# Causal attention of the second block: mask added to the forget sums by GpSimd, the minimum in two parts, reciprocals spread through memory

## The chip, the cores and the metric

The kernel runs on one core of one Trainium2 chip, and its time is the device time of one execution in microseconds (us). Three runs of the kernel before took 2592.71, 2601.61 and 2602.12 us; the median is 2601.61 us. The engines are named as in the profile: PE (TensorE, with PEld for its weight loads), DVE (VectorE), ACT (ScalarE), POOL (GpSimd) and SP (SyncE, which here only issues transfers).

## The reference

Two transformer blocks follow each other on 1024 tokens of width 1024, in float32: a first block with attention and a mixture of experts, and a second block with two attention layers. The change lies in the first layer of the second block, causal attention of 16 heads of 64 columns with forget gates:

```python
log_f = jax.nn.log_sigmoid((f_logit + b_forget[i]).astype(jnp.float32))
c = jnp.cumsum(log_f, axis=1)
...
logits = jnp.einsum('bqhd,bkhd->bhqk', qi, k) * scale
logits = logits + ci[..., :, None] - c_k[..., None, :]
causal = k_pos[None, :] <= q_pos[:, None]
logits = jnp.where(causal, logits, -jnp.inf)
p = jax.nn.softmax(logits, axis=-1)
return jnp.einsum('bhqk,bkhd->bqhd', p.astype(v.dtype), v)
```

The output o of a head is then multiplied by silu(gate), and goes into the layer's output projection. The term ci is the same for a whole row of the softmax and drops out of it, so that only the forget sums c_k of the keys have to be applied.

## The kernel before

The attention is one stage of a long program, in `fox_steps`; it lies at about 1774 to 2048 us of the profiled execution. Before it come the projections of q, k, v and gate (`mix_and_projection`), after it the output projection (`gated_out_norm_steps`), which begins on PE right behind the last product of the attention.

**Work.** The heads are taken two at a time (e = 0, 1 in the code), which makes eight head pairs; for each there are eight query tiles of 128 rows. One *pair* p of the code is one head pair and one tile, so there are 64 pairs (`NPAIR`). Tile t sees (t+1)*128 keys. The tiles of a head pair are taken in the order 0, 7, 1, 6, 2, 5, 3, 4 (the first head pair: 0, 1, 2, 7, 3, 6, 4, 5), a small tile and a large one in turn, and this document calls a run of eight pairs a cycle.

**Steps of one pair**, each engine working through its own program in order, with semaphores between them:

- PE, `scores`: for each of the two heads a product of identity and mask in bf16 (L3269) opens the accumulation in the 128 columns on the diagonal; then q times k (L3275) adds the scores, up to 512 columns at a time. It waits until DVE has read the scores of the pair before (`l_ready`), since all pairs use the same PSUM banks.
- DVE (L3245): for each head one pass over all (t+1)*128 columns computes scores*(-scale) + c into `fox_l` and the minimum of a row, `nbm`. The sums c lie in `fox_c`, spread over all partitions, two rows per head pair. The profile shows each pass as CUSTOM_DVE_ANT_0 and, behind it, DVE_READ_ACCUMULATOR2_ANT, which writes the minimum.
- ACT (L3181): the exponential with that minimum as its bias, and the sum of a row, `rsum`.
- DVE (L3258): the reciprocal of the two sums.
- POOL (L3192): copies the two reciprocals over 64 columns each, which makes a 128x128 tile in `pad`.
- PE (L3296): transposes the probabilities in 128x128 tiles into three PSUM banks (`transposes`), three steps later than the scores; ACT (L3169) copies the first four tiles to `fox_pt` and DVE (L3228) the others.
- PE, one step later: for every second pair two transposes of POOL's tiles (L3316), so that the reciprocals of a query lie in its column on 64 partitions per head; then v times the probabilities (L3325) into bank 7.
- DVE, for every second pair: copies the transposed reciprocals from PSUM to `pad` (L3217), waits for that copy, and multiplies the output by it (L3219); this frees bank 7 (`o_out`).
- POOL, after that: multiplies by the gate and splits the result into a rounded part and its rest (L3203, L3205, L3207), the operands of the output projection.

DVE's program in a step is: output of pair p-5 (if it is odd), copies of pair p-4, minimum of pair p, a piece of weight work in four steps, reciprocal of pair p-1. PE's is: transposes of the first four tiles of pair p-3, scores of pair p, values of pair p-4, the other transposes of pair p-3.

**Transfers of the stage.** SP issues them in order: two more rows of c (L3149), the 4 MB of gates G_a (L472), then one row of c after another as their slots come free, and between them 2 MB of weights of the next stage. All are on one queue, SP's.

## Time and profile before

| | us |
|---|---|
| median of three runs | 2601.61 |
| lowest and highest | 2592.71, 2602.12 |
| profiled execution, its own time | 2593.28 |
| span in its profile | 2591.5 |
| busy in the span: PE, DVE, ACT, POOL | 2472.0, 1651.5, 1371.9, 379.4 |
| busy in the stage, 1790 to 2045 us: PE, DVE, ACT, POOL | 245.06, 151.06, 159.86, 73.60 |

How to read the rows. A row by stretch holds the stretch and its length, then the busy us of PE, PEld, DVE, ACT and POOL with the number of instructions, the granted clock of PE (1.00 is full speed), the busy share of the DMA engines, and GB/s. A row of waits says who waited for whom, and then the us in total, how many times, and the longest. A row of the timeline begins with the start and the duration in us, names engine, line, operation, and output and inputs with their shapes; several instructions of one kind in a row are one row (x4: four), and brackets say how long the engine had been idle and for whom. A float32 product counts as two or more matmuls in these numbers. A row of DMA issues has the KB of one transfer and the median us from its issue to its landing; a queue's row has packets, MB, and the share of 16 engines' time.

### The profile page before, as it was taken

The page shows a single profiled execution, that of the slowest core. Times are in us where ns is not written, and L with a number is a line of the kernel's source. Part 1 is how long each engine was busy: PE and PEld are TensorE (multiplying, and loading weights), DVE is VectorE, ACT ScalarE, POOL GpSimd, SP SyncE. Part 2 cuts the span into 40 slices and gives each one's busy share as a digit, 9 for nine tenths or more (in the row PEclk, how much of TensorE's full clock was granted, in tenths as well). Part 3 has the DMA queues.
Part 4 walks back from the last instruction along what each step waited for, and adds up shares of the span by engine and source line. Part 5 has one row for each costly group of instructions (what it writes and reads, how often), then busy time and mean ns, then how long its engine had stood idle before and what let it go on. Part 6 is the DMA issues. An engine that isn't in the chain of part 4 may idle for free. (4 is left out here: it accounts for less than half of the span.)

```text
span 2591.5 us, 38243 instructions
## 1 busy us (share of the span) xinstructions
PE 2472.0 (95%) x13514; PEld 1979.2 (76%) x13526; DVE 1651.5 (64%) x3035; ACT 1371.9 (53%) x2421; POOL 379.4 (15%) x499
## 2 busy tenths in 40 slices
PE   6999999999987999999996999999999999999999
PEld 5788489788866888888885878886666787886667
DVE  5683455687668899999986655412556546742851
ACT  3352144697346788888885733323666433323850
POOL 0221121330301311111110000000232200000430
PEclk9999999999998999999998999999999999999999
DMA  7642000001229999999987511143020321113111
GB/s 250 187 139 85 1 1 1 1 1 57 93 114 392 420 410 415 417 413 410 416 326 264 178 37 66 33 134 129 31 73 27 113 80 70 33 54 145 63 50 49
DMA packets 129293, 400.26 MB, mean 154 GB/s; under 512 B 12135, under 2 KB 62572, under 8 KB 116734
## 3 DMA queue, kind: packets, MB, share of 16 engines
q1 hardware_dynamic: 117306, 359.79, 36.8%
q0 software_dynamic: 10736, 38.30, 3.7%
q8 instruction: 90, 1.47, 0.2%
q14 instruction: 53, 0.43, 0.1%
q10 hardware_dynamic: 1108, 0.27, 0.0%
HBM read 347.93 MB, written 50.40 MB: 154 GB/s over the span
## 5 line engine op out<-in xcount | busy, mean ns | idle before, releaser
L3245 DVE CUSTOM_DVE_ANT_0 fox_l<-PS,fox_c 128x384 f32<-128x384 f32 (+7 forms) x124 | 90.7, 768 | 82.7 <-PE PS L3275 81.7
L3181 ACT ACTIVATE fox_l<-fox_l,stat 128x384 f32<-128x384 f32 (+7 forms) x124 | 96.6, 781 | 79.6 <-DVE stat L3245 79.1
L3192 POOL COPY pad<-stat 128x128 f32<-128x128 f32 x64 | 18.7, 293 | 587.8 <-DVE stat L3258 587.6
L479 PE MATMUL PS<-wehg,xsTh 128*128 128x512 f32 x256 | 100.7, 393 | 3.6 <-ACT xsTh L2879 2.0
L479 PE MATMUL PS<-wehu,xsTh 128*128 128x512 f32 x256 | 103.6, 405 | 0.0
L479 PE MATMUL PS<-wqkh,uTh 128*128 128x512 f32 x256 | 103.0, 402 | 0.0
L481 PE MATMUL PS<-wehu,xsTl 128*128 128x512 f32 x256 | 100.8, 394 | 0.0
L481 PE MATMUL PS<-wehg,xsTl 128*128 128x512 f32 x256 | 100.5, 392 | 0.0
L481 PE MATMUL PS<-wqkh,uTl 128*128 128x512 f32 x256 | 100.2, 391 | 0.0
L480 PE MATMUL PS<-wqk_rest,uTh 128*128 128x512 f32 x256 | 99.9, 390 | 0.0
L481 PE MATMUL PS<-wehd,aTl 128*128 128x512 f32 x248 | 96.5, 389 | 0.0
L479 PE MATMUL PS<-wehd,aTh 128*128 128x512 f32 x248 | 96.5, 389 | 0.0
L479 PE MATMUL PS<-hTh,winh 128*128 128x512 f32 x208 | 85.3, 410 | 5.0 <-DVE hT_rest L381 3.4
L1499 DVE TENSOR_REDUCE stat<-PS 128x1 f32<-128x1024 f32 x64 | 78.1, 1224 | 17.8 <-PE PS L1536 14.3
L3296 PE MATMUL PS<-mats,fox_l 128*128 128x128 f32 x570 | 81.6, 280 | 6.1 <-DVE fox_pt L3228 4.2
L481 PE MATMUL PS<-hTh,win_rest 128*128 128x512 f32 x208 | 83.0, 399 | 0.0
L480 PE MATMUL PS<-hT_rest,winh 128*128 128x512 f32 x208 | 83.0, 399 | 0.0
L3275 PE MATMUL PS<-ka,qa 64*128 64x512 f32 (+3 forms) x384 | 81.1, 527 | 0.0
L2944 DVE TENSOR_TENSOR we0d_rest<-we0d,wehd 128x1024 fp32r<-128x1024 f32 x64 | 74.1, 1220 | 9.8 <-ACT wehd L2868 9.8
L3296 PEld LDWEIGHTS PS<-mats,fox_l 128*128 128x128 f32 x570 | 60.9, 140 | 23.0 <-issue 14.9
L2415 ACT ACTIVATE PS<-PS 128x512 f32<-128x512 f32 x32 | 18.6, 581 | 112.1 <-PE PS L481 112.1
L3325 PE MATMUL PS<-fox_pt,va 128*64 128x128 f32 x1152 | 77.0, 278 | 0.6 <-DVE fox_pt L3228 0.6
(626 smaller groups left out, 7558.2 us busy)
## 6 DMA issues: line engine op xcount, KB each, us to landing
we0g<-in_w_expert_gate SPq DMA_DIRECT2D x16, 2048.0 KB, 10.9
we0u<-in_w_expert_up SPq DMA_DIRECT2D x16, 2048.0 KB, 9.3
we1g<-in_w_expert_gate SPq DMA_DIRECT2D x16, 2048.0 KB, 11.2
we1u<-in_w_expert_up SPq DMA_DIRECT2D x16, 2048.0 KB, 9.8
we0d<-in_w_expert_down SPq DMA_DIRECT2D x16, 2048.0 KB, 10.3
we1d<-in_w_expert_down SPq DMA_DIRECT2D x16, 2048.0 KB, 10.5
wada_rest<-in_w_ada SPq DMA_DIRECT2D x16, 1024.0 KB, 6.6
X<-in_x SPq DMA_DIRECT2D x16, 512.0 KB, 7.9
```

What stands on the lines that cost most here:

```text
L479: nc.tensor.matmul(out, lh, rh, start=start, stop=False)
L480: nc.tensor.matmul(out, lh, rl, start=False, stop=False)
L481: return nc.tensor.matmul(out, ll, rh, start=False, stop=stop)
L1499: nc.vector.reduce_max(nb[:, w % 4:w % 4 + 1], bank(w), AX_X, negate=True).then_inc(nb_ready, 1)
L2415: nc.scalar.activation(PS[:, 3 + u % 2, :], PS[:, u % 3, :], ACT.Square).then_inc(squares, 1)
L2944: nc.vector.tensor_tensor(piece(wl[j][kind], kind, i), piece(w[j][kind], kind, i), piece(wh[kind], kind, i).bitcast(F32), ALU.subtract).th ...
L3181: nc.scalar.activation(prob(p, e)[:, 0:K], prob(p, e)[:, 0:K], ACT.Exp, bias=nbm[:, u % 8:u % 8 + 1], scale=-1.0, accum_out=rsum[:, u % 16 ...
L3192: nc.gpsimd.tensor_copy(rx(p).rearrange("p (e d) -> p e d", e=2), rsum[:, at:at + 2].unsqueeze(2).to_broadcast([P, 2, HD])).then_inc(rx_re ...
L3245: nc.vector.tensor_tensor_reduce(out=prob(p, e)[:, 0:K], in0=PS[:, 2 * e:2 * e + 2, :].rearrange("p a b -> p (a b)")[:, 0:K], in1=C[:, h % ...
L3275: last = nc.tensor.matmul(PS[:, 2 * e + n, 0:N], env.qa[r, c, t * P:(t + 1) * P], env.ka[r, c, n * HALF:n * HALF + N], start=(n != d), sto ...
L3296: last = nc.tensor.transpose(PS[:, 4 + at % NTB, (k % 4) * P:(k % 4 + 1) * P], prob(v, e)[:, k * P:(k + 1) * P], env.ident)
L3325: last = nc.tensor.matmul(PS[e * HD:(e + 1) * HD, 7, (w % 2) * P:(w % 2 + 1) * P], env.va[:, k, h * HD:(h + 1) * HD], PT[:, w % 2, e, k, : ...
```

## The change

- **Mask.** PE's two products with the mask are gone. GpSimd adds the mask to the 128 columns of c on the diagonal, for both heads in one instruction of 128x256 (L3221 of the changed kernel), into columns 256 to 511 of `pad`, up to two pairs ahead (`masked`).
- **Minimum in two parts.** DVE first passes over the 128 columns on the diagonal of both heads, with GpSimd's masked sums (L3269 of the changed kernel, result `nbd`). For tiles above 0 it then passes over the columns ahead of the diagonal of both heads, with c itself (L3278); the first minimum goes in as a scalar operand. A head's first pass is waited for with a semaphore (`diag_done`).
- **Reciprocals.** GpSimd's copy, PE's transposes and DVE's copy are gone. SP writes the reciprocals of two pairs, four columns of 128 partitions, to `r_dram`, turned so that a column becomes a row (L3175), waits for it (`r_saved`), and reads each head's rows back, spread over 64 partitions (L3182, two transfers), into columns 0 to 255 of `pad`. DVE's multiplication waits for them (`rb_in`).
- **Transfers.** The rows of c are loaded two at a time, at the start of a cycle, with one semaphore for two rows. The first 2 MB of the next stage's weights are issued at pair 32 as before, ahead of that pair's reciprocals.

On DVE the output and the minimum of a pair with tile 2 stood as follows, at the place where the profile has 1862.76 us (ISA with `fox_l` is a pass, ISA with `stat` alone the write of its minimum; pad_68 and pad_69 are the two buffers of `pad`):

```order
L3217 COPY pad_69<-PS 128x256
L3219 TENSOR_TENSOR qa<-PS,pad_69 128x256
L3245 ISA fox_l_7495,stat<-PS,fox_c 128x384
L3245 ISA stat 128x1
L3245 ISA fox_l_7495,stat<-PS,fox_c 128x384
L3245 ISA stat 128x1
L3258 RECIPROCAL stat<-stat 128x2
L3228 COPY fox_pt<-PS 128x512 x2
```

The same place of the changed kernel:

```order
L3243 TENSOR_TENSOR qa<-PS,pad_69 128x256
L3269 ISA fox_l_7495,stat<-PS,pad_68 128x128
L3269 ISA stat 128x1
L3269 ISA fox_l_7495,stat<-PS,pad_68 128x128
L3269 ISA stat 128x1
L3278 ISA fox_l_7495,stat<-PS,fox_c,stat 128x256
L3278 ISA stat 128x1
L3278 ISA fox_l_7495,stat<-PS,fox_c,stat 128x256
L3278 ISA stat 128x1
L3291 RECIPROCAL stat<-stat 128x2
L3253 COPY fox_pt<-PS 128x512 x2
```

One copy ahead of the multiplication is gone; two passes over 384 columns became four, over 128 and 256.

On SP, at the beginning of the stage, the program before goes from the gates straight on to the rows of c, each behind its own wait:

```order
L3149 DMA fox_c<-c_dram 128x1024 x2
L472 DMA G_a<-g_dram 128x8x1024
L3149 DMA fox_c<-c_dram 128x1024 x7
L472 DMA wo_a<-in_w_out_a 128x8x512
L3149 DMA fox_c<-c_dram 128x1024 x5
```

The changed kernel, from the same place, up to the next two rows of c:

```order
L3158 DMA fox_c<-c_dram 128x1024 x2
L472 DMA G_a<-g_dram 128x8x1024
L3175 DMA r_dram<-stat 128x4x1
L3182 DMA pad_68<-r_dram 64x2x128 x2
L3175 DMA r_dram<-stat 128x4x1
L3182 DMA pad_69<-r_dram 64x2x128 x2
L3175 DMA r_dram<-stat 128x4x1
L3182 DMA pad_68<-r_dram 64x2x128 x2
L3175 DMA r_dram<-stat 128x4x1
L3182 DMA pad_69<-r_dram 64x2x128 x2
L3158 DMA fox_c<-c_dram 128x1024 x2
```

Between the rows of c of two cycles there are now four writes and eight reads, and the first write stands right behind the gates.

The diff:

```diff
-    env.C, env.c_in = m.at("fox_c", 11, [P, 4, S]), [sem(f"c_in{i}") for i in range(4)]
+    env.C, env.c_in = m.at("fox_c", 11, [P, 4, S]), [sem(f"c_in{i}") for i in range(2)]
...
             gate_chunk(c)
         sp.wait_ge(c_saved, 16)
         for h in range(2):
-            sp.dma_start(env.C[:, h, :], env.c_dram[h, :].partition_broadcast(P)).then_inc(env.c_in[h], 16)
+            sp.dma_start(env.C[:, h, :], env.c_dram[h, :].partition_broadcast(P)).then_inc(env.c_in[0], 16)
         sp.wait_ge(mm, 4 * T)
         for t in range(T):
             sp.dma_start(env.va[:, t, :], env.v_dram[t * P:(t + 1) * P, :]).then_inc(va_in, 16)
...
     C, c_in = env.C, env.c_in
-    nbm, rsum = env.stat[:, 0:8], env.stat[:, 8:24]
+    nbm, rsum, nbd = env.stat[:, 0:8], env.stat[:, 8:24], env.stat[:, 24:32]
+    causal = env.mats[:, 6 * P:7 * P]
     s_ready, l_ready, exp_done, r_ready = sem("fox_s"), sem("fox_l"), sem("fox_exp"), sem("fox_r")
-    t_ready, pt_first, pt_second, pv_done, rb_out, o_out = (sem("fox_t"), sem("fox_ptA"), sem("fox_ptD"), sem("fox_pv"),
-                                                            sem("fox_rb"), sem("fox_oo"))
-    rx_ready, gate_step, o_lo = sem("fox_rx"), sem("gate_a"), sem("o_lo_a")
+    t_ready, pt_first, pt_second, pv_done, o_out = (sem("fox_t"), sem("fox_ptA"), sem("fox_ptD"), sem("fox_pv"),
+                                                    sem("fox_oo"))
+    masked, diag_done, r_saved, rb_in = sem("fox_masked"), sem("fox_diag"), sem("fox_r_saved"), [sem(f"fox_rb{i}") for i in range(2)]
+    gate_step, o_lo = sem("gate_a"), sem("o_lo_a")
...
         return first[p][:, e, :] if p < 2 else Lr[p % 4 // 2][:, p % 2, e, :]
-    def rx(w):
-
-        at = (2 + w // 2 % 2) * P
-        return env.pad[w % 2][:, at:at + P]
+    def rb(i):
+
+        return env.pad[i % 2][:, 0:2 * P]
+
+    def diagonal(p):
+
+        return env.pad[p % 2][:, 2 * P:4 * P].rearrange("p (e k) -> p e k", e=2)
+
+    def diagonals_before(p):
+
+        return sum(2 for q in range(p) if tile_of(q))
     def chunks_before(p):
...
         a, b = order(w)[w % T - 1], order(w)[w % T]
         return x[:, w // T, :].rearrange("p (t q) -> p t q", q=P)[:, a:b + 1:b - a, :]
+
+    def score(e):
+
+        return PS[:, 2 * e:2 * e + 2, :].rearrange("p a b -> p (a b)")
     def both(x):
...
     def on_sp(sp):
-        for h in range(2, NH):
-            if h >= 4:
-
-                sp.wait_ge(l_ready, 2 * T * (h // 2 - 1))
-            elif h == 2:
-                sp.wait_ge(env.ag_mm, 2 * KD - 2)
-            sp.dma_start(C[:, h % 4, :], env.c_dram[h, :].partition_broadcast(P)).then_inc(c_in[h % 4], 16)
-            if h == 3:
-                sp.wait_ge(env.ag_mm, 2 * KD)
-                for i in range(2):
-                    sp.wait_ge(env.ag_saved[i], 16 * KD)
-                load(sp, [env.G])
-            if h == NH // 2 + 2:
-                sp.wait_ge(s_ready, NPAIR)
+        def c_rows(c):
+            for h in (2 * c, 2 * c + 1):
+                sp.dma_start(C[:, h % 4, :], env.c_dram[h, :].partition_broadcast(P)).then_inc(c_in[c % 2], 16)
+
+        sp.wait_ge(env.ag_mm, 2 * KD - 2)
+        c_rows(1)
+        sp.wait_ge(env.ag_mm, 2 * KD)
+        for i in range(2):
+            sp.wait_ge(env.ag_saved[i], 16 * KD)
+        load(sp, [env.G])
+        for i in range(NPAIR // 2):
+            w = 2 * i
+            if w % T == 0 and 1 <= w // T < NH // 2 - 1:
+                sp.wait_ge(l_ready, 2 * w)
+                c_rows(w // T + 1)
+            if w == NPAIR // 2:
                 load(sp, env.wo_a[0:1])
+            at = 2 * w % 16
+            sp.wait_ge(r_ready, w + 2)
+            sp.dma_start(env.r_dram[i % 2, :, :].rearrange("x q -> q x"),
+                         rsum[:, at:at + 4],
+                         allow_slow_non_contiguous=True).then_inc(r_saved, 16)
+            sp.wait_ge(r_saved, 16 * (i + 1))
+            if i >= 2:
+                sp.wait_ge(o_out, i - 1)
+            for e in range(2):
+                sp.dma_start(both(rb(i)[e * HD:(e + 1) * HD, :]),
+                             env.r_dram[i % 2, e::2, :].partition_broadcast(HD)).then_inc(rb_in[i % 2], 16)
     def on_act(act):
         for p in range(NPAIR + LAG):
...
                                          accum_out=rsum[:, u % 16:u % 16 + 1]).then_inc(exp_done, 1)
     def on_pool(pool):
+        pool.wait_ge(env.qk_out, 4 * T)
         for p in range(NPAIR + LAG + 2):
             if p < NPAIR:
-                at = 2 * p % 16
-                pool.wait_ge(r_ready, p + 1)
-                if p >= 4:
-                    pool.wait_ge(pv_done, p - 3)
-                nc.gpsimd.tensor_copy(rx(p).rearrange("p (e d) -> p e d", e=2),
-                                      rsum[:, at:at + 2].unsqueeze(2).to_broadcast([P, 2, HD])
-                                      ).then_inc(rx_ready, 1)
+                h = 2 * (p // T) % 4
+                if p % T == 0:
+                    pool.wait_ge(c_in[p // T % 2], 32 * (p // T // 2 + 1))
+                if p >= 2:
+                    pool.wait_ge(l_ready, 2 * p - 2)
+                at = tile_of(p) * P
+                nc.gpsimd.tensor_tensor(diagonal(p), C[:, h:h + 2, at:at + P],
+                                        causal.unsqueeze(1).to_broadcast([P, 2, P]), ALU.add).then_inc(masked, 1)
             w = p - LAG - 2
             if w < 0 or w % 2 == 0:
                 continue
...
         for p in range(NPAIR + LAG + 2):
             w = p - LAG - 2
             if w >= 0 and w % 2:
-                rb = both(env.pad[w // 2 % 2][:, 0:2 * P])
+                dve.wait_ge(rb_in[w // 2 % 2], 32 * (w // 4 + 1))
                 dve.wait_ge(pv_done, w + 1)
-                if w >= 4:
-                    dve.wait_ge(o_out, w // 2 - 1)
-                nc.vector.tensor_copy(rb, both(PS[:, 7, 2 * P:4 * P])).then_inc(rb_out, 1)
-                dve.wait_ge(rb_out, w // 2 + 1)
-                nc.vector.tensor_tensor(two(env.qa, w), both(PS[:, 7, 0:2 * P]), rb, ALU.mult).then_inc(o_out, 1)
+                nc.vector.tensor_tensor(two(env.qa, w), both(PS[:, 7, 0:2 * P]), both(rb(w // 2)), ALU.mult
+                                        ).then_inc(o_out, 1)
             v = p - LAG - 1
             if 0 <= v < NPAIR and tile_of(v) >= 4:
                 nk = tile_of(v) + 1 - 4
...
                                           PS[:, 4 + (chunks_before(v) + 2 + e) % NTB, 0:nk * P]
                                           ).then_inc(pt_second, 1)
             if p < NPAIR:
-                K = (tile_of(p) + 1) * P
+                D = tile_of(p) * P
+                if p == 4:
+                    for i in range(2):
+                        dve.wait_ge(env.ag_saved[i], 16 * KD)
+                dve.wait_ge(masked, p + 1)
                 for e in range(2):
                     u = 2 * p + e
-                    h = 2 * (p // T) + e
-                    if p % T == 0:
-                        dve.wait_ge(c_in[h % 4], 16 * (h // 4 + 1))
-                    if p == 4 and e == 0:
-                        for i in range(2):
-                            dve.wait_ge(env.ag_saved[i], 16 * KD)
                     dve.wait_ge(s_ready, u + 1)
                     if p >= 4:
                         dve.wait_ge(t_ready, chunks_before(p - 3))
+                    to = (nbd if D else nbm)[:, u % 8:u % 8 + 1]
                     nc.vector.tensor_tensor_reduce(
-                        out=prob(p, e)[:, 0:K], in0=PS[:, 2 * e:2 * e + 2, :].rearrange(
-                            "p a b -> p (a b)")[:, 0:K], in1=C[:, h % 4, 0:K], scale=-FSCALE, scalar=3.0e38,
-                        op0=ALU.add, op1=ALU.min, accum_out=nbm[:, u % 8:u % 8 + 1]).then_inc(l_ready, 1)
+                        out=prob(p, e)[:, D:D + P], in0=score(e)[:, D:D + P], in1=diagonal(p)[:, e, :], scale=-FSCALE,
+                        scalar=3.0e38, op0=ALU.add, op1=ALU.min, accum_out=to).then_inc(diag_done if D else l_ready, 1)
+                for e in range(2 if D else 0):
+                    u = 2 * p + e
+                    h = 2 * (p // T) + e
+                    if p % T == 1:
+                        dve.wait_ge(c_in[p // T % 2], 32 * (p // T // 2 + 1))
+                    dve.wait_ge(diag_done, diagonals_before(p) + e + 1)
+                    nc.vector.tensor_tensor_reduce(
+                        out=prob(p, e)[:, 0:D], in0=score(e)[:, 0:D], in1=C[:, h % 4, 0:D], scale=-FSCALE,
+                        scalar=nbd[:, u % 8:u % 8 + 1], op0=ALU.add, op1=ALU.min, accum_out=nbm[:, u % 8:u % 8 + 1]
+                        ).then_inc(l_ready, 1)
             if p - 1 in HALF_AT:
                 j = HALF_AT.index(p - 1)
                 dve.wait_ge(env.w_hi_a, j + 1)
...
             pe.wait_ge(l_ready, 2 * p)
         d = t // 4
-        at = (t % 4) * P
-        for e in range(2):
-            nc.tensor.matmul(PS[:, 2 * e + d, at:at + P], env.identb[:, :], env.masksb[:, 0:P],
-                             start=True, stop=False, skip_group_check=True)
         for n in range(d + 1):
             N = min(HALF, K - n * HALF)
             for e in range(2):
                 r = slice(e * HD, (e + 1) * HD)
                 last = nc.tensor.matmul(PS[:, 2 * e + n, 0:N], env.qa[r, c, t * P:(t + 1) * P],
                                         env.ka[r, c, n * HALF:n * HALF + N],
-                                        start=(n != d), stop=True, skip_group_check=True)
+                                        start=True, stop=True, skip_group_check=True)
                 if n == d:
                     last.then_inc(s_ready, 1)
...
             if 0 <= w < NPAIR:
                 c, t = w // T, tile_of(w)
                 if w % 2 == 0:
-                    pe.wait_ge(rx_ready, w + 2)
                     if w >= 2:
                         pe.wait_ge(o_out, w // 2)
-                    for i in range(2):
-                        nc.tensor.transpose(PS[:, 7, (2 + i) * P:(3 + i) * P], rx(w + i), env.ident)
                 if w == 0:
                     pe.wait_ge(env.va_in, 16 * T)
                 pe.wait_ge(pt_first, 2 * w + 2)
...
     env.c_dram = nc.dram_tensor("c_dram", (NH, S), F32, kind="Internal").ap()
+    env.r_dram = nc.dram_tensor("r_dram", (2, 4, P), F32, kind="Internal").ap()
```

## Rows read from the trace of the kernel before

**Rows 1.** Busy time by stretch, whole stage (us; busy by engine, clock, DMA)

```profile
1790.00:2045.00 255.00, 245.06 (x2261) 168.47 (x2262) 151.06 (x436) 159.86 (x382) 73.60 (x155) 0.99 0.16 54
```

**Rows 2.** Waits in the stage (us in total, times, longest)

```profile
DVE fox_l L3245 <- PE PS L3275: 81.7, 54, 4.1
...
PEld PS L3269 <- DVE stat L3245: 6.2, 16, 1.8
```

**Rows 3.** Timeline of one step on TensorE (start, us, engine, line)

```profile
1847.42 0.28 PE L3269 MATMUL PS<-masksb,identb 128*128 128x128 bf16 x2
...
1847.63 0.49 PE L3275 MATMUL PS<-ka,qa 64*128 64x128 f32 x4
...
1848.05 0.44 PE L3316 MATMUL PS<-mats,pad 128*128 128x128 f32 x2
...
1848.42 0.88 PE L3325 MATMUL PS<-fox_pt,va 128*64 128x128 f32 x12
```

**Rows 4.** Timeline: VectorE's minimum, 128 and 1024 columns, twice each

```profile
1848.25 0.29 DVE L3245 CUSTOM_DVE_ANT_0 fox_l<-PS,fox_c 128x128 f32<-128x128 f32 x1 [0.75 <-PE PS L3275]
...
1848.47 0.29 DVE L3245 CUSTOM_DVE_ANT_0 fox_l<-PS,fox_c 128x128 f32<-128x128 f32 x1
...
1852.96 1.23 DVE L3245 CUSTOM_DVE_ANT_0 fox_l<-PS,fox_c 128x1024 f32<-128x1024 f32 x1 [2.50 <-PE PS L3275]
...
1854.11 1.22 DVE L3245 CUSTOM_DVE_ANT_0 fox_l<-PS,fox_c 128x1024 f32<-128x1024 f32 x1
```

**Rows 5.** Timeline where TensorE and VectorE meet (idle before in brackets)

```profile
1842.27 1.02 DVE L3228 COPY fox_pt<-PS 128x384 f32<-128x384 f32 x2
...
1842.94 0.31 PEld L3296 LDWEIGHTS PS<-mats,fox_l 128*128 128x128 f32 x3 [0.29 <-issue]
...
1855.39 0.11 PEld L3269 LDWEIGHTS PS<-masksb,identb 128*128 128x128 bf16 x2 [0.21 <-DVE stat L3245]
...
1858.07 0.49 DVE L3228 COPY fox_pt<-PS 128x128 f32<-128x128 f32 x2 [0.88 <-PE PS L3296]
...
1865.32 1.29 DVE L3228 COPY fox_pt<-PS 128x512 f32<-128x512 f32 x2 [0.21 <-PE PS L3296]
```

**Rows 6.** Timeline of VectorE: a reciprocal, and the copy using it

```profile
1857.04 0.16 DVE L3258 RECIPROCAL stat<-stat 128x2 f32<-128x2 f32 x1
...
1870.11 0.42 DVE L3217 COPY pad<-PS 128x256 f32<-128x256 f32 x1
```

**Rows 7.** Timeline: GpSimd's gate ends, and VectorE's next minimum

```profile
1857.01 0.73 POOL L3207 TENSOR_TENSOR qa_rest<-qa,oh_a 128x256 fp32r<-128x256 f32 x1
...
1860.65 1.09 DVE L3245 CUSTOM_DVE_ANT_0 fox_l<-PS,fox_c 128x896 f32<-128x896 f32 x1 [2.09 <-PE PS L3275]
```

**Rows 8.** DMA issues (KB, us to landing); a queue in 0 to 30

```profile
G_a<-g_dram SPq DMA_DIRECT2D x1, 4096.0 KB, 15.5
...
wr<-in_w_router_expert SPq DMA_DIRECT2D x1, 128.0 KB, 2.7
...
c_dram<-F SPq DMA_DIRECT2D x1, 64.0 KB, 1.9
...
bf<-in_b_forget SPq DMA_DIRECT2D x1, 0.1 KB, 10.5
...
q10 hardware_dynamic: 1108, 0.27, 4.0%
```

**Rows 9.** GB/s in 1 us slices from 1786; timeline of SP

```profile
GB/s 0 14 305 164 225 356 422 422 422 414 422 418 406 418 410 406 266 16 16 0 0 0 0 0 0 16 0 135 266 315 320 12 0 0 0 0 0 0 16 0
...
1789.63 0.37 SPq L472 DMA_DIRECT2D G_a<-g_dram  x1
```

**Rows 10.** Timeline: VectorE's first copy, and TensorE's values behind it

```profile
1804.15 0.40 DVE L3217 COPY pad<-PS 128x256 f32<-128x256 f32 x1
...
1806.07 0.88 PE L3325 MATMUL PS<-fox_pt,va 128*64 128x128 f32 x12
```

**Rows 11.** Busy time by stretch, early in the stage

```profile
1790.00:1796.00 6.00, 5.15 (x14) 2.03 (x14) 1.88 (x6) 1.88 (x9) 0.29 (x1) 0.50 1.01 377
```

## The prediction

> **What bounds the kernel now.** I read the busy time by stretch first. In the stage of the change, 255 us of the span, PE is busy for 245.06 us, DVE for 151.06, ACT for 159.86 and POOL for 73.60, at a clock of 0.99 [rows 1]. So an instruction less on PE counts there unless PE then waits, and the waits say for whom it would. DVE's passes waited 81.7 us for PE's scores, but PE's weight load of the mask also waited 6.2 us, 16 times, for DVE's minimum [rows 2]. Sixteen in eight cycles is two in a cycle, and the timeline shows the places: behind the scores of the two largest tiles PE is done with everything else and stands until both minima are there, as at 1855.39 for 0.21 us [rows 5]. There DVE leads. PE has to be watched at a second kind of meeting too, where its transposes wait for a bank that DVE's copy of probabilities frees. So the stage is bound by PE, with places in every cycle that DVE sets.
>
> **What PE loses.** *The mask.* From the first of the two mask products to the first score 0.21 us pass (1847.42 to 1847.63), and from the transposes of the reciprocals to the first value product 0.37 us (1848.05 to 1848.42) [rows 3]. The mask stands ahead of the scores of every pair, between DVE's minimum of one pair and its minimum of the next, so its time counts wherever either engine leads: 64 x 0.21 = 13.4 us. The transposes stand in 32 steps, those of the small tiles: 32 x 0.37 = 11.8 us of PE work, which counts only where PE still leads afterwards.
>
> **What DVE gains and loses.** A minimum of 128 columns starts 0.22 us after the one before it (1848.25, 1848.47), one of 1024 columns 1.15 us after (1852.96, 1854.11) [rows 4]. That is 0.93 us for 896 columns, 1.04 ns a column, and leaves 0.09 us that a pass costs at any width. Dividing a head's pass adds that once, 0.17 us a pair of two heads. The scalar operand and the wait between a head's two passes do not occur in this trace. The upper bound is that each added pass costs a whole small one, 0.22 a head and 0.44 a pair; nothing less than the fixed part can be had, since the columns stay the same. I take 0.20, next to the lower end, because the other head's first pass lies between a head's two passes and covers the wait. DVE's copy of the reciprocals and the wait for it go, from 1870.11 about 0.46 us in every second step, but DVE then only waits that much longer for the small tile's scores: I count nothing. ACT starts its exponential some 0.3 us later behind the largest tiles; it is busy 159.86 of 255 us, and its copies are due a step later, so I count nothing here either.
>
> **Where they meet, in one cycle** [rows 5].
> - Behind tiles 7 and 6 PE already waits for the minimum (1855.39). The wait grows by 0.20: 16 x 0.20 = 3.2 us lost.
> - Behind tile 3 DVE goes from minimum and reciprocal straight to its copy (1842.27, no idle time ahead of it), and PE's last weight loads wait for that copy (1842.94, idle 0.29). DVE leads: 8 x 0.20 = 1.6 us lost, and the 0.37 of the transposes only lengthens the wait.
> - Behind tile 2 DVE's copy (1865.32) waited 0.21 us for PE. With DVE 0.20 later and PE 0.37 earlier, 0.01 is left: nothing gained.
> - Behind tiles 0 and 1 DVE waited 0.88 us (1858.07; the other is like it). 0.88 - 0.37 - 0.20 = 0.31, so PE still leads and the transposes count: 16 x 0.37 = 5.9 us.
> - Tiles 4 and 5 have no transposes behind them, and PE leads.
>
> Sum of the steady stage: 13.4 + 5.9 - 3.2 - 1.6 = 14.5 us gained. With 0.17 a pair it is 15.2, with 0.44 it is 6.8 (24 places lose 0.44, and tile 2's eight lose 0.23 as well).
>
> **GpSimd.** Its copy of 128 columns is replaced by an addition over 256, like the 0.73 us of the gate's last part, which at 1857.01 ends at 1857.74. The masked sums of the next pair stand behind a gate, so they would be ready at 1858.5; DVE needs them at 1860.65 [rows 7]. Up to 2.1 us of cover, so nothing is charged; without it, the minimum and then PE's next scores would be late.
>
> **The reciprocals through memory.** The last reciprocal of a group ends at 1857.20 and is used at 1870.11 [rows 6]: 12.9 us, less four shortened steps of 0.23 us, leaves 12.0. The way: the write to memory like the 64 KB of c_dram, 1.9 us. It consists of 512 single floats, 32 on each of 16 engines; the queue with the small packets shows 4.0% of 16 engines over 30 us for 1108 packets, 17 ns each, so 0.6 more. Two reads of 64 KB each, issued 0.4 us apart, like wr's 128 KB, 2.7 us [rows 8]. With 0.1 for SP that is 5.7 us, below 12.0: hidden. Bounds are 1.9 + 1.9 = 3.8 and, if the write takes what the 0.1 KB of bf took, 10.5 + 0.4 + 2.7 = 13.6. In the Trainium skill, "DMA: Bandwidth & Descriptors", Rules for kernel authors, a strided last dimension becomes one descriptor per element; the count of 512 above is the same, and no run yet shows such a write alone.
>
> **The first group is not hidden.** SP issues the 4 MB of gates at 1789.63 [rows 9], and the first write stands right behind them on the same queue. The bytes flow until about 1802.6 (the slice from 1802 has 266 GB/s, the next 16) [rows 9]. If the write waits for them, it lands at 1802.6 + 0.6 + 1.9 = 1805.1 and the reads at about 1808.2; the multiplication ends at 1808.6. DVE's copy stood at 1804.15, and PE's values, which need bank 7 free, at 1806.07 [rows 10]; with five masks (1.05) and 0.37 saved PE would be there at 1804.65. It waits 4.0 us. That small transfers wait behind large ones shows in bf, 10.5 us for 0.1 KB issued behind loads of megabytes [rows 8]. The Trainium skill, same page, Queues, rings and completion order, has each DMA engine take a ring's descriptors in order; bf's row agrees, and with the rule the start costs what stands here, without it nothing.
> After an idle stretch the clock was at 0.50 from 1790 to 1796 [rows 11], half of that time 3.0 us of full-speed work; a stall may bring this again, and I add 1.0. Together 5.0 us. Bounds: 0, if the write passes the gates and the reads are there by 1796, and 9.5, if it starts only when the gates have landed (15.5 us after their issue, 1805.1) and the clock takes its 3.0.
>
> **Sum.** 14.5 - 5.0 = 9.5 us gained; everything behind the stage is started by its last products and moves with them. The profiled execution took 2593.28, so it would be 2583.8. Two of three runs shown are 9 us above it; the difference goes on the median: 2601.61 - 9.5 = 2592.1. Own range from the bounds: gains of 15.2 - 0 to losses of 9.5 - 6.8, 2586 to 2604. About 0.5%, 13 us, is what a measurement of this kernel can tell from no change.
>
> **Rivals.**
> - *PE keeps all of it.* The transposes and masks save 25.2 us, and DVE, without its copy, is early enough at every meeting. For it: DVE is busy 59% of the stage. Against it: the waits of rows 5. With half the start's loss 2579; with none 2576.
> - *The round trip is late.* From 12.0 us on, DVE stands before a multiplication with passes and copies queued behind it, and PE stands behind DVE. A delay in one group moves the next group's deadline as well, so it is paid once in four steps, some 15 times. With the 13.6 us of the upper bound: 15 x 1.6 = 24 us, 24 - 9.5 = 14.5 slower, 2616; 14 us would give 2622. For it: bf's row and the writes of single floats. Against it: c_dram's 1.9, and that only 54 GB/s flow over the stage [rows 1].
> - *DVE leads everywhere.* What PE loses turns into waits for the longer minimum, nothing is gained, and the start costs its 5.0: 2607. Against it: DVE's 81.7 us of waiting for PE.
>
> **Chances.** Forecast 0.56, PE keeps all 0.20, round trip late 0.12, DVE leads everywhere 0.12. Faster by over 0.5% (below 2589): the first rival and 0.10 of the forecast's share, 0.30. Slower: the late round trip and a little of the rest, 0.13. Within: 0.57. The range of 8 in 10 takes in the first rival nearly whole and the third: 2577 to 2610.
>
> **What would show it.** In the changed profile: steps of DVE's passes 0.17 to 0.2 us longer for a pair; PE waiting some 0.4 behind tiles 7 and 6, and longer behind tiles 2 and 3; a landing of about 2.5 us for the write and 2.7 for the reads; one wait of DVE for the first reads near 1804, of some 4 us, and none for later ones. The prediction is wrong if DVE waits for reads in most cycles, if POOL's masked sums are what passes wait for, or if no wait behind tiles 2 and 3 appears.

## The result and the profile after

The changed kernel took 2724.48 us (median of four runs, 2719.33 to 2726.53), the kernel before 2597.72 us; the ratio is 1.0486 with an interval of 1.0456 to 1.0515. It is slower by 4.9%, and the forecast of 2592.1 us (2577 to 2610) was wrong. The profiled execution took 2726.53 us, its span is 2724.7 us.

The same stretch as in [rows 1], from 1790 us to the end of the stage, and the start:

```profile
1790.00:1796.00 6.00, 4.83 (x12) 1.89 (x12) 2.10 (x10) 1.65 (x7) 0.72 (x1) 0.50 1.02 402
...
1808.00:1814.00 6.00, 1.73 (x13) 1.40 (x14) 2.20 (x10) 1.03 (x2) 1.49 (x3) 0.62 0.19 22
...
1790.00:2172.00 382.00, 262.45 (x2076) 180.87 (x2076) 152.97 (x621) 160.59 (x380) 98.35 (x153) 0.83 0.21 47
```

DVE and ACT are as busy as before, but the stage takes 382 us where it took 255, and PE's granted clock, 0.99 before, is 0.83. PE stands idle again and again (from 1868 to 1872 us it is busy for 0.19 us of 4), and behind some of the pauses its granted clock is 0.50, the lower of its two levels (from 1872 to 1876 us; 0.62 in the stretch shown from 1808). At that clock the same work counts as more busy time: 16 transposes take 3.68 us at 0.50 and 2.16 at 1.00 (both below).

Who waits for whom, first of the engines, then of SP's queue (these answer to [rows 2]; in total, how many times, the longest):

```profile
DVE qa L3243 <- DMA pad<-r_dram: 126.8, 23, 11.6
...
PE PS L3351 <- DVE qa L3243: 102.1, 23, 10.4
...
DVE fox_l L3269 <- PE PS L3304: 54.1, 21, 4.0
```

```profile
SPq L3182 <- DMA r_dram<-stat: 301.3, 31, 17.6
...
SPq L3175 <- DVE stat L3291: 4.6, 5, 1.7
```

DVE's multiplication waits for the reciprocals, and PE's next values wait for that multiplication. The chain goes on to SP: it waits 9.7 us for each write to be in memory (9.5 without the first, 17.6, which stands behind the gates), and hardly ever for the reciprocals. So the group is there before SP comes to it. SP's own timeline shows the beat:

```profile
1858.69 0.60 SPq L3175 DMA_DIRECT2D r_dram<-stat  x1
1867.28 1.22 SPq L3182 DMA_DIRECT2D pad<-r_dram  x2
1868.54 0.59 SPq L3175 DMA_DIRECT2D r_dram<-stat  x1
1878.84 1.22 SPq L3182 DMA_DIRECT2D pad<-r_dram  x2
1880.11 0.59 SPq L3175 DMA_DIRECT2D r_dram<-stat  x1
```

A write, 8 to 10 us until it is in memory, two reads, and at once the next write: 9.9 and 11.6 us from one write to the next, each for two pairs. DVE's output (count, durations in ns, first and last start), before and after, shows what the engines would have needed:

```profile
L3219 DVE TENSOR_TENSOR qa<-PS,pad x32: 424/424/426, 1804.6 to 2048.0; 128x256 f32<-128x256 f32 x32
```

```profile
L3243 DVE TENSOR_TENSOR qa<-PS,pad x32: 401/423/425, 1811.8 to 2182.3; 128x256 f32<-128x256 f32 x32
```

Before, 31 steps took 243.4 us, 7.85 us each; after, 370.5 us, 11.95 us each. 31 x 4.10 = 127.1 us. The first output comes 7.2 us later (7.9 if one counts from DVE's first pass of the stage, 1774.5 us before and 1773.8 after, since executions differ a little ahead of it). Together that is 134.3 us; the spans differ by 133.2. So the loss is in this beat and its start. I use this distance, first output to last, for every kernel below and call it the *steady part*.

The transfers (KB, us from issue to landing; they answer to [rows 8], and the write has no landing of its own in this view):

```profile
fox_c<-c_dram SPq DMA_DIRECT2D x16, 512.0 KB, 5.4
...
pad<-r_dram SPq DMA_DIRECT2D x64, 64.0 KB, 3.7
...
r_dram<-stat SPq DMA_DIRECT2D x32, 2.0 KB
```

A write of 2 KB (9.7 us of waiting) takes longer than a load of 512 KB (5.4).

### The profile page after: what moved, and what is told of

Read it like the earlier page. It is cut to its first block and busy times, and to the rows that moved or that the text cites. A ratio compares the mean times of both kernels' runs of the same rounds, so it can differ in the third digit from the quotient of the medians.

```text
span 2724.7 us, 38156 instructions
## 1 busy us (share of the span) xinstructions
PE 2494.1 (92%) x13334; PEld 1993.2 (73%) x13334; DVE 1653.2 (61%) x3227; ACT 1372.2 (50%) x2421; POOL 401.8 (15%) x499
## 3 DMA queue, kind: packets, MB, share of 16 engines
q1 hardware_dynamic: 143418, 364.05, 36.4%
## 5 line engine op out<-in xcount | busy, mean ns | idle before, releaser
L3351 PE MATMUL PS<-fox_pt,va 128*64 128x128 f32 x1152 | 86.9, 301 | 102.6 <-DVE qa L3243 102.1
L3351 PEld LDWEIGHTS PS<-fox_pt,va 128*64 128x64 f32 x1152 | 68.8, 149 | 132.9 <-DVE qa L3243 115.1
L3325 PE MATMUL PS<-mats,fox_l 128*128 128x128 f32 x570 | 100.1, 329 | 9.9 <-DVE fox_pt L3253 8.7
L3221 POOL TENSOR_TENSOR pad<-fox_c,mats 128x256 f32<-128x256 f32 x64 | 45.3, 727 | 422.2 <-ACT ka L2406 327.8
L3325 PEld LDWEIGHTS PS<-mats,fox_l 128*128 128x128 f32 x570 | 78.8, 168 | 27.2 <-issue 20.7
L3304 PE MATMUL PS<-ka,qa 64*128 64x512 f32 (+3 forms) x384 | 90.1, 577 | 9.4 <-DVE stat L3278 8.6
L3243 DVE TENSOR_TENSOR qa<-PS,pad 128x256 f32<-128x256 f32 x32 | 13.4, 418 | 126.8 <-DMA pad<-r_dram 126.8
L3269 DVE CUSTOM_DVE_ANT_0 fox_l<-PS,pad 128x128 f32<-128x128 f32 x124 | 31.0, 286 | 85.5 <-PE PS L3304 54.1
## 6 DMA issues: line engine op xcount, KB each, us to landing
we1g<-in_w_expert_gate SPq DMA_DIRECT2D x16, 2048.0 KB, 11.3
we0d<-in_w_expert_down SPq DMA_DIRECT2D x16, 2048.0 KB, 10.5
```

What stands on the lines that cost most here:

```text
L3221: nc.gpsimd.tensor_tensor(diagonal(p), C[:, h:h + 2, at:at + P], causal.unsqueeze(1).to_broadcast([P, 2, P]), ALU.add).then_inc(masked, 1)
L3269: nc.vector.tensor_tensor_reduce(out=prob(p, e)[:, D:D + P], in0=score(e)[:, D:D + P], in1=diagonal(p)[:, e, :], scale=-FSCALE, scalar=3.0 ...
L3304: last = nc.tensor.matmul(PS[:, 2 * e + n, 0:N], env.qa[r, c, t * P:(t + 1) * P], env.ka[r, c, n * HALF:n * HALF + N], start=True, stop=Tr ...
L3325: last = nc.tensor.transpose(PS[:, 4 + at % NTB, (k % 4) * P:(k % 4 + 1) * P], prob(v, e)[:, k * P:(k + 1) * P], env.ident)
L3351: last = nc.tensor.matmul(PS[e * HD:(e + 1) * HD, 7, (w % 2) * P:(w % 2 + 1) * P], env.va[:, k, h * HD:(h + 1) * HD], PT[:, w % 2, e, k, : ...
```

## The experiments

In every diff the lines are against the changed kernel, unless it says otherwise.

### Each part of the change alone

The old way of the reciprocals, with GpSimd's masks and the minimum in two parts kept:

```diff
-            sp.dma_start(env.r_dram[i % 2, :, :].rearrange("x q -> q x"), rsum[:, at:at + 4], ...)
-            sp.dma_start(both(rb(i)[...]), env.r_dram[i % 2, e::2, :].partition_broadcast(HD))
+            nc.gpsimd.tensor_copy(rx(v + i)..., rsum[:, at:at + 2].unsqueeze(2).to_broadcast([P, 2, HD]))
+            nc.tensor.transpose(PS[:, 7, (2 + i) * P:(3 + i) * P], rx(w + i), env.ident)
+            nc.vector.tensor_copy(both(rb(0)), both(PS[:, 7, 2 * P:4 * P]))
```

> The changed kernel with the reciprocals spread as before (GpSimd's copy, PE's transposes, DVE's copy); mask by GpSimd and the minimum in two parts stay. Theory A (the stage is paced by SP, which does one write, its wait and two reads after the other, 11.6 us for every two pairs): without the round trip the loss is gone. What is left is 13.4 us of mask products gained less 24 x 0.2 us of longer minima: 8.6 us faster than before, about 2589. Rival B (the passes of the minimum or GpSimd's masked sums carry a good part of the loss): at least 30 us slower than before, 2630 or more.

Measured: 2600.79 us against 2599.82, ratio 1.0006 (0.9991 to 1.0022). The loss is gone, so it comes from the reciprocals' way through memory. But the gain that I expected of the masks isn't there either. Its waits:

```profile
DVE fox_l L3277 <- POOL pad L3217: 23.5, 13, 2.1
...
PEld PS L3312 <- DVE stat L3286: 12.6, 16, 2.5
```

The first is this kernel's own: GpSimd has the old copies to make again, and its masked sums come late 13 times. The second answers to the 6.2 us of [rows 2]: PE's scores wait longer for the minimum in two parts.

The counterpart, reciprocals through memory, PE's mask and the minimum in one pass as before:

```diff
-                nc.gpsimd.tensor_tensor(diagonal(p), C[:, h:h + 2, at:at + P], causal..., ALU.add)
+            nc.tensor.matmul(PS[:, 2 * e + d, at:at + P], env.identb[:, :], env.masksb[:, 0:P], ...)
```

> The reciprocals through memory alone; PE's mask products and the minimum in one pass as before, no masked sums on GpSimd. Theory A: SP's loop paces the stage whatever PE and DVE do, so it is as slow as the changed kernel within 6 us, 2718 to 2730. Rival B: the loss is divided between the parts, and this one is below 2690.

Measured: 2725.57 us, ratio 1.0485 (1.0454 to 1.0516), the same as the whole change. SP waits as there:

```profile
SPq L3182 <- DMA r_dram<-stat: 313.8, 32, 19.0
```

### What makes the write slow

The same 2 KB as 128 runs of 16 bytes, one of each partition, in place of 512 single floats:

```diff
-            sp.dma_start(env.r_dram[i % 2, :, :].rearrange("x q -> q x"), rsum[:, at:at + 4],
-                         allow_slow_non_contiguous=True).then_inc(r_saved, 16)
+            sp.dma_start(env.r_dram[i % 2, :, :], rsum[:, at:at + 4]).then_inc(r_saved, 16)
```

> The changed kernel with the write in 128 runs of 16 bytes, one behind the other, in place of 512 single floats; the reads take the same bytes in the order in which they lie, so the reciprocals that the output is multiplied by are permuted. Theory A1 (the 9.7 us from a write's issue to its end belong to the 512 single floats): the write takes 2 to 4 us, SP's loop 4 to 6, below the 8 us of two pairs, and the time is 2585 to 2597 with the start's loss. Rival A2 (any write to memory that is waited for takes so long here): 9 to 10 us a write, 2715 to 2730.

Measured: 2594.87 us, ratio 0.9982 (0.9967 to 0.9997). SP now waits for reciprocals more than for writes (its waits), and the write lands in 1.4 us (the transfers behind):

```profile
SPq L3175 <- DVE stat L3290: 119.1, 30, 6.6
...
SPq L3180 <- DMA r_dram<-stat: 60.0, 32, 13.7
```

```profile
pad<-r_dram SPq DMA_DIRECT2D x64, 64.0 KB, 2.9
...
r_dram<-stat SPq DMA_DIRECT2D x32, 2.0 KB, 1.4
```

The loss hangs on the form of the write alone, not on the trip through memory. The queue's packets agree with the count of 512 floats: SP's queue has 143418 of them in the changed kernel and 131130 in this one, 384 fewer for each of 32 writes, which is 512 less 128. This kernel is also the best look at my other terms, below.

512 single floats again, but each 512 bytes from the next:

```diff
-            sp.dma_start(env.r_dram[i % 2, :, :].rearrange("x q -> q x"),
+            sp.dma_start(env.far_dram[i % 2, :, 0:1].rearrange("(q x) a -> q (x a)", x=4),
```

> The changed kernel, its write still 512 single floats, but each float 512 bytes from the next in memory (before, neighbours lay side by side); the reads, same number and size, take other data (rows of c), so the output is multiplied by other numbers. Theory P (each separately written float costs time of its own): a write still takes 9 to 10 us, time 2710 to 2730. Rival L (it is the crowding: 16 engines write single floats into the same few hundred bytes): the write falls below 4 us and the time to 2585 to 2605.

A quarter of the floats, one column of 128, side by side as in the change:

```diff
-            sp.dma_start(env.r_dram[i % 2, :, :].rearrange("x q -> q x"), rsum[:, at:at + 4],
+            sp.dma_start(env.r_dram[i % 2, 0:1, :].rearrange("x q -> q x"), rsum[:, at:at + 1],
```

> The changed kernel writing one of the four columns, 128 single floats side by side in place of 512; the reads take other data (rows of c), so the output is multiplied by other numbers. Theory P: 128 floats cost a quarter of 8 us above the 1.4 us that runs of 16 bytes took, 3 to 4 us a write; SP's loop is below 8 us and the time 2585 to 2600. Rival F (a write with single floats costs about 9 us whatever their number): 2710 to 2730.

512 floats, 8 bytes apart, one partition's four behind the other's:

```diff
-    env.far_dram = nc.dram_tensor("far_dram", (2, 4 * P, P), F32, kind="Internal").ap()
+    env.far_dram = nc.dram_tensor("far_dram", (2, 4 * P, 2), F32, kind="Internal").ap()
```

(against the kernel with 512 bytes)

> The changed kernel, but its write puts the 512 single floats 8 bytes apart, partition after partition, into 4 KB: each of 16 engines has its own stretch of 256 bytes and shares it with no other, yet the floats lie close together. The reads fetch rows of c of the same size instead, so the output is multiplied by other values. Theory S: what costs 8 us is that several engines put single floats into the same few tens of bytes (with the floats 512 bytes apart a write took 2.1 us, one of 128 bytes' runs or of 16 byte runs 1.4). Then this write lands in 1.4 to 2.5 us, SP waits 60 to 80 us in 32 waits, and the ratio is 0.998 to 1.002. Theory B: single floats close to each other in memory are slow whichever engine brings them. Then SP waits for 8 to 10 us each time, some 260 to 310 us in all, and the ratio is 1.035 to 1.05.

Measured, in the same order: ratios 0.9991 (0.9976 to 1.0007), 1.0361 (1.0332 to 1.0391) and 1.0055 (1.0035 to 1.0074). The second, 2689.45 us, lies in neither range of its expectation. The rows that decide are the transfers and SP's waits of the kernel with 512 bytes, SP's waits in the one with 128 floats, and both again of the one with 8 bytes:

```profile
far_dram<-stat SPq DMA_DIRECT2D x32, 2.0 KB, 2.1
...
SPq L3182 <- DMA far_dram<-stat: 70.7, 32, 13.7
```

```profile
SPq L3182 <- DMA r_dram<-stat: 262.1, 32, 16.5
```

```profile
far_dram<-stat SPq DMA_DIRECT2D x32, 2.0 KB, 4.7
...
SPq L3182 <- DMA far_dram<-stat: 150.8, 32, 14.4
```

To compare like with like, take SP's mean wait for a write, without the first, which stands behind the gates: 9.5 us in the change, 7.9 for 128 floats side by side, 4.4 at 8 bytes, 1.8 at 512 bytes, and 1.5 with runs of 16 bytes. 512 floats far apart are quick, so a price for each float is excluded. 128 floats side by side take nearly as much as 512. At 8 bytes neither of my two theories holds as put: the landing of 4.7 us lies between them. That kernel and the one with 512 bytes differ in the distance alone, and there the shorter distance costs 2.6 us a write. Against the change they differ in a second thing: there the neighbours of a float come from neighbouring partitions, here the four floats of one partition follow each other. So how much of the step from 9.5 to 4.4 us is distance isn't shown. The steady part follows the write: 370.5 us in the change, 327.2 with 128 floats, 249.8 at 8 bytes and 238.0 at 512. At 8 bytes SP's round is 4.4 + 1.2 + 0.6 = 6.2 us, below the 7.85 of the engines, and DVE's output waits in five places only, 20.7 us in all.

The wait grows with how close single floats lie, far more than with how many there are. Runs of 16 bytes lie just as dense, as many of them as there are floats in the second kernel, and are quick; so it is not density alone, but single floats close together. What in the path of the write makes it so isn't shown, nor how the floats are divided over the DMA engines.

### Does it help to keep two writes under way?

From the kernel with the reciprocals alone; SP issues a group's write before it waits for the one before (only the wait is shown). The reads of a group so stand behind the next group's write, and behind SP's wait for that group's reciprocals:

```diff
-            sp.wait_ge(r_saved, 16 * (i + 1))
+            k = i - 1
+            sp.wait_ge(r_saved[k % 2], 16 * (k // 2 + 1))
```

> The kernel of the run before last (reciprocals through memory alone) with SP issuing the next write before it waits for the last one, so that two writes are under way. Theory A (SP's loop in series is what paces): SP can then follow two pairs in 8 us, and only the length of the trip, 9.7 + 1.2 + 3.6 = 14.5 us against 12 to 13, remains, once in four steps: 16 x 2 us, less 6 of PE's transposes: 2615 to 2640. Rival C (what counts is a trip's length against its due time, and that SP works in series adds nothing): no better than the reciprocals alone in series, within 10 us.

Measured: 2704.94 us, ratio 1.0408 (1.0378 to 1.0439). Little comes back, which neither side expected:

```profile
fox_c<-c_dram SPq DMA_DIRECT2D x16, 512.0 KB, 12.2
...
pad<-r_dram SPq DMA_DIRECT2D x64, 64.0 KB, 7.8
...
r_dram<-stat SPq DMA_DIRECT2D x32, 2.0 KB, 8.8
```

```profile
SPq L3176 <- DVE stat L3276: 287.6, 32, 13.0
```

Reads that stand behind the next write on the queue now take 7.8 us, and rows of c 12.2 instead of 5.4. A transfer behind such a write is held up with it. The other half is the new order: SP now hardly waits for writes (15.4 us), but 287.6 us for reciprocals. The next write is issued as soon as DVE has its reciprocals, the reads behind it land 7.8 us later, DVE's multiplication waits for them, and only behind that multiplication does DVE make the reciprocals of the group after (multiplication at 1858.35, reciprocals at 1859.64, the write at 1859.83). One beat has become another, of 349.3 us in the steady part where the changed kernel has 370.5. So this run doesn't test the serial loop cleanly; reads ahead of the next write, or on another queue, weren't tried.

### What the masks are worth

GpSimd's masks for the tiles 0, 1, 4 and 5 only, one pair earlier; PE's mask and one pass for the others; reciprocals as before:

```diff
+    SPLIT = (0, 1, 4, 5)
...
-                    if p >= 2:
-                        pool.wait_ge(l_ready, 2 * p - 2)
+                    if nth(n) >= 2:
+                        pool.wait_ge(l_ready, 2 * [q for q in range(n) if split(q)][-2] + 2)
```

> Reciprocals spread on chip as in the kernel before; GpSimd's mask and the minimum in two parts only for tiles 0, 1, 4 and 5, behind which VectorE had 0.9 us and more to spare; tiles 2, 3, 6 and 7 keep PE's mask and one pass. GpSimd makes the masked sums one pair earlier than in the first experiment. Theory D (the longer minimum, 0.38 us a pair as the trace of the run with 16-byte runs shows, costs only where VectorE leads): 32 x 0.21 = 6.7 us gained and none lost, 0.9974 of before. Rival (the masked sums or the longer exponential chain cost as much as the mask): 1.000 to 1.002.

Measured: 2599.31 us against 2596.01, ratio 1.0011 (1.0000 to 1.0022), where I expected a gain; the steady part is 243.5 us, before 243.4. That is the rival's range; what takes the gain of these masks isn't shown. So I left PE's mask out altogether, with nothing in its place (against the kernel before):

```diff
-            nc.tensor.matmul(PS[:, 2 * e + d, at:at + P], env.identb[:, :], env.masksb[:, 0:P],
-                             start=True, stop=False, skip_group_check=True)
-                                        start=(n != d), stop=True, skip_group_check=True)
+                                        start=True, stop=True, skip_group_check=True)
```

> The kernel before without PE's mask products, and with nothing in their place: the 128 columns on the diagonal are not masked, all else is as before. It measures what the two products are worth on PE's path. Forecast's term: 64 x 0.21 = 13.4 us, a ratio of 0.9948 (range 0.994 to 0.9957). Rival: from the last transposes of a pair to the next scores PE took 1.85 us with the mask and 1.74 without it in the run with four tiles, from 8 transposes 1.14 and 1.02, so that a removed mask is worth 0.12, since the first weight load of the scores then shows; 64 x 0.12 = 7.7 us, a ratio of 0.997 (range 0.9962 to 0.998). Neither would hold if DVE's minimum sets the pace behind the scores of most tiles: then 0.999 to 1.0005.

Measured: 2587.82 us against 2593.53, ratio 0.9983 (0.9970 to 0.9996): 4.4 us by the ratio, and 7.8 at most; the steady part is 237.5 us, 5.9 less than before. The forecast's 13.4 us are excluded. The timeline says why. First PE before, then without the mask, from the transposes ahead of tile 7 to its scores, and a cycle of eight pairs:

```profile
1913.86 1.99 PE L3275 MATMUL PS<-ka,qa 64*128 64x512 f32 x8
...
1943.61 1.67 PE L3296 MATMUL PS<-mats,fox_l 128*128 128x128 f32 x12
1945.12 0.28 PE L3269 MATMUL PS<-masksb,identb 128*128 128x128 bf16 x2
1945.33 1.99 PE L3275 MATMUL PS<-ka,qa 64*128 64x512 f32 x8
```

```profile
1904.87 1.67 PE L3293 MATMUL PS<-mats,fox_l 128*128 128x128 f32 x12
1906.47 1.99 PE L3272 MATMUL PS<-ka,qa 64*128 64x512 f32 x8
...
1911.87 0.41 PE L3313 MATMUL PS<-mats,pad 128*128 128x128 f32 x2 [0.24 <-DVE qa L3219]
...
1937.12 1.99 PE L3272 MATMUL PS<-ka,qa 64*128 64x512 f32 x8
```

From transposes to scores PE takes 1.72 us with the mask and 1.60 without it. The 0.21 us from mask to scores [rows 3] are there, but when the mask goes, 0.09 to 0.10 of them stay. A cycle is 31.47 us before and 30.65 without the mask, 0.82 for eight pairs: 0.10 a mask, half of my term. Part of what PE wins turns into a new wait, as the 0.24 us for DVE's output.

### Versions that mend the write

DVE turns the reciprocals of a group in 32x32 blocks, so that the write has 16 runs of 128 bytes; the gates are loaded behind the first group. First on top of the four tiles, then with PE's mask and one pass for all:

```diff
+                nc.vector.reciprocal(rr[:, 2 * (q % 2):2 * (q % 2) + 2], rsum[:, c]).then_inc(r_ready, 1)
+                    nc.vector.transpose(rt, rr).then_inc(r_ready, 1)
...
+            for b in range(4):
+                sp.dma_start(env.r_dram[i % 2, :, 32 * b:32 * b + 32], rt[32 * b:32 * b + 4, :]).then_inc(r_saved, 16)
```

> As the run before this one, but with the reciprocals through memory: VectorE turns 32x32 blocks, so that SP writes 16 runs of 128 bytes in four transfers in place of 512 floats, and the gates are loaded behind the first group. Theory: a write's wait is 1.5 to 3 us, SP's loop below 7 us, no multiplication waits in a usual cycle; 6.7 us from four masks, 16 x 0.37 behind tiles 0 and 1 and 8 x 0.21 behind tile 2, 14 us in all less up to 3 at the start: 0.9945 to 0.997 of before. Rival (transfers late again, or PE's saved transposes all turn into waits): 0.997 to 1.05.

> The reciprocals through memory alone, turned on DVE by its 32x32 transposition into 16 runs of 128 bytes, and the gates loaded behind the first group; the mask stays PE's and the minimum one pass. What is open: the run with turned reciprocals and GpSimd's masks for four tiles took 0.9980 [0.9967, 0.9993] of the kernel before, the same masks with the old reciprocals 1.0011 [1.0000, 1.0022]. If the gain is the reciprocals' alone (theory R), this one loses neither passes nor gate order to the masks and keeps 16 x 0.37 = 5.9 us behind tiles 0 and 1, more behind tiles 2 and 3 where DVE's copy of 0.40 us is gone and no split is in the way (up to 16 x 0.2 = 3.2), less 1 to 2 us of DVE's turning of 32 groups and the start: 4 to 8 us, a ratio of 0.997 to 0.9985, SP waiting some 40 us in 32 waits for its writes. If masks and reciprocals need each other (theory M: PE, quicker behind the transposes, only waits for DVE's minimum and nothing but a shorter step by the mask turns it into time), the ratio is 0.9995 to 1.0015, with PE's weight loads of the mask waiting for DVE longer than the 6.2 us of before.

Measured: ratios 0.9980 (0.9967 to 0.9993) and 0.9971 (0.9957 to 0.9985), the latter 2589.64 us against 2598.23. The first falls short of its theory's 0.9945 to 0.997. The second is the best of the versions that compute the layer as it stands, and has none of the masks, so the gain doesn't need them. Its output, SP's wait, PE's waits, and one of DVE:

```profile
L3234 DVE TENSOR_TENSOR qa<-PS,pad x32: 401/404/426, 1802.3 to 2040.8; 128x256 f32<-128x256 f32 x32
```

```profile
SPq L3178 <- DMA r_dram<-dest: 42.8, 32, 8.0
```

```profile
PE PS L3319 <- DVE fox_pt L3244: 12.1, 16, 2.5
```

```profile
1807.76 0.21 DVE L3281 STREAM_TRANSPOSE dest<-stat 128x32 f32<-128x32 f32 x1 [2.18 <-DMA r_dram<-dest]
```

The steady part is 238.5 us, 4.9 less than before. PE's row shows where the rest of the transposes' 11.8 us went: PE waits for DVE's copies of probabilities, 12.1 us, and before 4.2. The longest of these waits, 2.5 us, is not a usual one. The second group's write now stands behind the gates (SP's longest wait, 8.0 us), DVE waits 2.18 us for it before it turns the next, and its copies come late. Without this one wait the steady part would be some 7.4 us shorter than before, by my estimate.

## Why the prediction was wrong, step by step

**The step that failed: "the round trip through memory, 5.7 us, below 12.0: hidden".** I priced the write at 1.9 us from c_dram's row and 0.6 for 512 packets at 17 ns. The floats' number was right (the packets show 512); it wasn't what costs. The write took 8 to 10 us, 9.7 in the mean, and that comes with its floats side by side: the same data in runs of 16 bytes landed in 1.4 us, the same number of floats 512 bytes apart in 2.1.

**The rival had the late trip, but the wrong price.** From the write at 1858.69 to the reads' landing (issued 1867.28 and 0.6 later, 3.7 on the way) the trip takes some 12.9 us, inside my bounds of 3.8 to 13.6. I let it be "paid once in four steps, some 15 times", as if groups could overlap. They don't: one SP program writes, waits and reads for a group before it takes the next. So the bound is not the 12.0 us of one group's margin, but the 7.85 us in which the engines make a group, against 9.7 + 1.2 + 0.6 = 11.5 us of SP. The upper bound that I had in hand, 10.5 us for bf, would have given 31 x (10.5 + 1.8 - 7.85) = 138 us by that reckoning, near the truth; I wrote 24.

**The mask, 13.4 us: mis-sized.** 64 x 0.10 = 6.4 us by the cycles of the kernel without it, 5.9 in its steady part, 4.4 by the ratio of the times.

**The split of the minimum, 0.20 us a pair: mis-sized.** The timeline of the kernel with 16-byte runs, tile 7, first DVE, then PE (with tiles 3 and 6 as well):

```profile
1855.74 0.29 DVE L3268 CUSTOM_DVE_ANT_0 fox_l<-PS,pad 128x128 f32<-128x128 f32 x1 [2.49 <-issue]
...
1856.19 1.15 DVE L3277 CUSTOM_DVE_ANT_0 fox_l<-PS,fox_c,stat 128x896 f32<-128x896 f32 x1
...
1857.26 1.15 DVE L3277 CUSTOM_DVE_ANT_0 fox_l<-PS,fox_c,stat 128x896 f32<-128x896 f32 x1
...
1858.33 0.08 DVE L3277 DVE_READ_ACCUMULATOR2_ANT stat<- 128x1 f32 x1
```

```profile
1846.37 0.52 PE L3324 MATMUL PS<-mats,fox_l 128*128 128x128 f32 x3 [0.67 <-DVE fox_pt L3252]
...
1858.47 0.70 PE L3303 MATMUL PS<-ka,qa 64*128 64x256 f32 x4 [0.37 <-DVE stat L3277]
...
1865.69 0.92 PE L3303 MATMUL PS<-ka,qa 64*128 64x384 f32 x4 [0.30 <-DVE stat L3277]
```

From the first pass to the end of the last minimum it is 2.67 us, where two passes over 1024 columns took 2.38 (1852.96 to 1855.34, from [rows 4]). That is 0.29 more: 0.17 for two more passes, and two passes of 896 columns with the first minimum as an operand take 1.07 each, start to start, where the kernel before takes 1.02 for 896 columns (1860.65 to 1861.67). The first pass also starts later, 0.19 us behind PE's values (1855.55) and not 0.10 (1852.86). So it is 0.38, near the upper bound of 0.44. The places were right: PE waits 0.37 behind tile 7 and 0.30 behind tile 6 for the minimum, and 0.67 behind tile 3 for DVE's copies, as forecast. Behind tile 2, where I left 0.01, it waits 0.47 (at 1868.86). 24 x 0.38 = 9.1 us lost instead of 4.8, more than the mask's 6.4: the masks with the old reciprocals had a steady part of 245.7 us, 2.3 more than before.

**The transposes, 5.9 us: nearly right.** With PE's mask kept and the reciprocals mended, 4.9 us, or some 7.4 without the one wait behind the gates; on top of the four tiles 243.5 - 237.6 = 5.9 us, with a like wait of 1.9 us in it.

**The start, 5.0 us: right in kind, and in size by some luck.** Again with 16-byte runs, the timelines of SP, DVE and PE (they answer to [rows 9 to 11]):

```profile
1790.22 0.32 SPq L3175 DMA_DIRECT2D r_dram<-stat  x1
1804.24 1.34 SPq L3180 DMA_DIRECT2D pad<-r_dram  x2
```

```profile
1807.63 0.42 DVE L3242 TENSOR_TENSOR qa<-PS,pad 128x256 f32<-128x256 f32 x1 [2.74 <-DMA pad<-r_dram]
```

```profile
1808.11 1.55 PE L3350 MATMUL PS<-fox_pt,va 128*64 128x128 f32 x12 [1.90 <-DVE qa L3242]
1809.59 3.68 PE L3324 MATMUL PS<-mats,fox_l 128*128 128x128 f32 x16
```

The first write waits behind the gates. From DVE's first pass of the stage to the first output it is 34.0 us (1773.64 to 1807.63), before 30.1 (1774.52 to 1804.58), and 31.9 with the masks and the old reciprocals. So the output is 3.9 us late, of which 1.8 are there with masks and split alone; that leaves 2.1 for the transfers. PE itself waits 1.90 and not my 4.0. The 16 transposes then take 3.68 us at a granted clock of 0.50 from 1808 to 1812, behind 4 us in which PE was busy for 1.35; the kernel before takes 2.16 for them (1806.88), at a clock of 1.00. That is 1.5 more, 5.4 in all. The changed kernel, with the slow write added, is at 1811.8. With the gates behind the first group the first output is on time (29.8 us), but the wait only moves to the second group, as shown above.

**GpSimd's masked sums, no charge: right.** With 16-byte runs a pass waits for them once, for 2.1 us.

**The sum.** The mask was 7.0 us too good, the split 4.3; 14.5 - 11.3 leaves 3.2 us, and the steady part with 16-byte runs is 4.9 us shorter than before (238.5). With a write as cheap as I assumed, the change takes 0.9982 (0.9967 to 0.9997) of the time before; my forecast was 2592.1 / 2601.61 = 0.9963.

## What to carry to other kernels

Where one queue's program serves groups in series, compare the time of its whole round with the time in which the engines make a group, not only one trip with one group's margin; then price the upper bound by that. A transfer of many single floats to neighbouring addresses has to be measured or avoided: turn the data on the chip first, or write one run per partition. A small write behind a bulk load waits for it, and moving the load can move the wait to the next group. An instruction removed ahead of a product is worth what the next start moves, which here was half of the time between the two starts.

## What the runs showed of the hardware

- SP's mean wait for a write, without the first: 9.5 us for 512 floats side by side, 7.9 for 128 of them, 4.4 for 512 at 8 bytes apart, 1.8 at 512 bytes; 1.5 for 2 KB in 128 runs of 16 bytes. The Trainium skill, "VectorE: DVE Perf Modes", The three transpose paths, warns of a plain DMA copy that transposes by strides when the innermost destination stride is large. In the change and in the kernel with 512 bytes that stride is the same, 512 bytes, and the waits are 9.5 and 1.8 us: here the stride alone doesn't decide. No run has the path with which the page compares.
- Transfers behind such a write on the same queue wait with it: reads land in 7.8 us instead of 3.7, 512 KB in 12.2 instead of 5.4.
- A pass of DVE with the first minimum as an operand per partition was 0.05 us longer than one without: 1.07 and 1.02 us at 896 columns, 0.27 and 0.22 at 128.

Open: why closeness costs what it does, and what the order of the floats adds to it; why the masks of four tiles gain nothing; and in the masks with the old reciprocals, how the 23.5 us of waits for GpSimd share in the 2.3 us lost.
